# Attention scores with the low key products in two row halves of TensorE, and a choice table built from two small ones

## The reference

```
s_c   = q @ kcmp  - slope * dist      # 127 compressed keys, softmax, gives the importance of blocks
sel   = top 8 of 32 blocks of 64 keys # first block, own block and the one before are forced
s_sel = q @ k     - slope * (t - key) # softmax over the chosen blocks, key <= t
s_win = q @ k     - slope * (t - key) # softmax over a window of 512 keys
o     = gate0 * o_cmp + gate1 * o_sel + gate2 * o_win
```

## Time and profile before

| | us |
|---|---|
| median of 3 runs | 4977.47 |
| range of the runs | 4975.93 to 4987.32 |
| the profiled execution's own time | 4984.44 |
| its span, first to last instruction | 4982.9 |
| TensorE busy in the span | 4327.2 (87%) |
| VectorE busy | 2748.0 (55%) |
| GpSimd busy | 729.3 (15%) |
| attention, from 2022.4 to 3077.3 us of the span | 1054.9 |

### The profile page before, as it was taken

The page is one execution under the profiler, slowest core; times in us unless marked ns, Lnnn a source line. Parts: engine busy times, 40 slices in busy tenths (PEclk is TensorE's granted clock), DMA queues, the critical chain, the costliest instruction groups (busy, mean ns, idle before and its releaser), DMA issues. The chain is left out here.

```text
span 4982.9 us, 66879 instructions
## 1 busy us (share of the span) xinstructions
PE 4327.2 (87%) x24608; PEld 3592.7 (72%) x24609; DVE 2748.0 (55%) x4353; ACT 2039.0 (41%) x3193; POOL 729.3 (15%) x599
## 2 busy tenths in 40 slices
PE   6999999999999995788888876799635999999699
PEld 5887887888788773566666764688534888888577
DVE  2655655556567562576666654443225654557465
ACT  2433332233223221455555553101225655557465
POOL 0111111111122130211111110000012100001110
PEclk9999999999999997899999986899657999999899
DMA  4332322233222214000000001423217865669742
GB/s 138 108 87 74 107 81 62 86 109 87 65 74 61 67 43 104 25 11 14 17 15 17 14 22 55 140 94 115 92 59 293 314 249 214 245 256 344 286 145 98
DMA packets 440438, 558.72 MB, mean 112 GB/s; under 512 B 38908, under 2 KB 299004, under 8 KB 439148
## 3 DMA queue, kind: packets, MB, share of 16 engines
q1 hardware_dynamic: 387892, 451.51, 27.6%
q0 software_dynamic: 19072, 59.86, 3.2%
q10 hardware_dynamic: 33232, 44.10, 2.7%
HBM read 445.05 MB, written 110.35 MB: 111 GB/s over the span
## 5 line engine op out<-in xcount | busy, mean ns | idle before, releaser
L434 POOL TENSOR_TENSOR fr_Lm<-fr_M,fr_join 128x512 f32<-128x512 f32 x224 | 370.9, 1673 | 1493.2 <-DVE fr_M L1043 963.4
L462 PE MATMUL fr_fb<-fr_hT_h,fr_w_h 128*128 128x512 f32 (+1 forms) x1312 | 528.3, 403 | 16.6 <-DVEq L1004 10.8
L462 PE MATMUL fr_fb<-fr_hT_r,fr_w_h 128*128 128x512 f32 (+1 forms) x1312 | 527.4, 402 | 0.0
L462 PE MATMUL fr_fb<-fr_hT_h,fr_w_r 128*128 128x512 f32 (+1 forms) x1312 | 526.3, 401 | 0.0
L855 DVE TENSOR_TENSOR fr_w_r<-fr_w_raw,fr_w_h 128x1024 fp32r<-128x1024 f32 (+1 forms) x164 | 209.6, 1278 | 409.7 <-ACT fr_w_h L683 409.4
L1781 DVE TENSOR_TENSOR aq_p_lo<-aq_t_bank,aq_p_hi 128x512 fp32r<-128x512 f32 x412 | 281.4, 690 | 271.5 <-ACT aq_p_hi L1671 270.1
L1671 ACT CAST aq_p_hi<-aq_t_bank 128x512 fp32r<-128x512 f32 x412 | 238.9, 585 | 377.5 <-PE aq_t_bank L1585 375.4
L707 ACT COPY fr_zs<-fr_fb 128x512 f32<-128x512 f32 (+1 forms) x148 | 87.0, 588 | 585.0 <-PE fr_fb L462 584.6
L462 PEld LDWEIGHTS fr_fb<-fr_hT_h,fr_w_h 128*128 128x128 f32 (+1 forms) x1312 | 246.9, 188 | 74.7 <-DVEq L1004 11.3
L134 PE MATMUL ex_gu<-ex_gate_w,ex_xT 128*128 128x512 f32 x1176 | 288.3, 401 | 11.5 <-DVE ex_xT L2407 11.4
L134 PE MATMUL ex_yps<-ex_down_w,ex_hidT 128*128 128x512 f32 x1176 | 287.6, 400 | 2.6 <-DVE ex_hidT L2423 2.6
(11 more groups left out here) (438 smaller groups left out, 9957.8 us busy)
## 6 DMA issues: line engine op xcount, KB each, us to landing
ex_raw<-in_w_exp_gate_up SPq DMA_DIRECT2D x64, 2048.0 KB, 10.9
fr_w_raw<-in_w_in SPq DMA_DIRECT2D x160, 512.0 KB, 3.8
ex_raw<-in_w_exp_down SPq DMA_DIRECT2D x32, 2048.0 KB, 11.1
s_z<-fr_zs SPq DMA_DIRECT2D x160, 256.0 KB
s_rows<-ex_y ACTq DMA_DIRECT2D x50, 512.0 KB, 4.3
mx_mg<-s_z SPq DMA_DIRECT2D x16, 1024.0 KB, 7.8
fr_zc<-s_z SPq DMA_DIRECT2D x15, 903.0 KB, 6.8
fr_x_t<-in_x SPq DMA_DIRECT2D x16, 512.0 KB, 4.8
```

The costliest lines, as they stand in the source:

```text
L434: pool.tensor_tensor(Lm[:, g, :, :], M[:, 4 * g:4 * g + 4, 0, :], join[:, lev:lev + 1, :].to_broadcast([P, HG, CH]), ALU.mult).then_inc(l_ ...
L462: ins = pe.matmul(bank[0:cols_, :], (w_h, w_h, w_r)[p][:, k, c, 0:cols_].bitcast(F32R), (hT_h, hT_r, hT_h)[p][:, c, :].bitcast(F32R), star ...
```

## The change

It does four things. (1) The scores of a run are cut into two halves of equal width, one for each PSUM bank, where before they were cut into pieces of 512 and a remainder. (2) The products with `k_hi` stay over 128 rows. Those with `k_lo` are taken over 64 rows, with the rounded queries only: the first half of the keys from partitions 0 to 63, the second from 64 to 127, so that (q_lo)(k_lo) is no longer computed and the two products use different row halves of the array and different banks. (3) They need the rounded queries in all 128 partitions: a new tile `q_hh`, for which `take_q` makes one more rounding copy (64x1024). (4) The long table `t_sel` goes. `bias` now adds `sel` to a row of 32 numbers (`base`), adds that to a 128x64 table (`near`), and masks the last 128 keys by a select. VectorE's `mask` reads the two banks as two halves.

```diff
+            q_hh = st.sb("q_hh", [P, 2, G, R, P])
...
-                    pool.tensor_copy(whole(q_s, every).bitcast(F32R), raw(every)).then_inc(q_high, 1)
-                    pool.wait_ge(q_high, o + 1)
-                    pool.tensor_tensor(whole(q_s, rest).bitcast(F32R), raw(rest), whole(q_s, rest), ALU.subtract).then_inc(q_ok, 1)
+                    pool.tensor_copy(whole(q_hh, every).bitcast(F32R), raw(every)).then_inc(q_high, 1)
+                    pool.tensor_copy(whole(q_s, top_).bitcast(F32R), raw(top_)).then_inc(q_high, 1)
+                    pool.wait_ge(q_high, 2 * o + 2)
+                    pool.tensor_tensor(whole(q_s, rest).bitcast(F32R), raw(rest), whole(q_hh, rest), ALU.subtract).then_inc(q_ok, 1)
...
+                    pool.tensor_tensor(base[:, 0:blocks], ramp[:, N_SEL - blocks:N_SEL], sel[:, f % SELS, 0:blocks], ALU.add).then_inc(base_ok, 1)
+                    pool.wait_ge(base_ok, 2 * f + 1)
                     pool.tensor_tensor(tg[:, 0:keys].rearrange("p (n b) -> p n b", n=blocks),
-                                       t_sel[:, S - t * P:S - t * P + keys].rearrange("p (n b) -> p n b", n=blocks),
-                                       sel[:, f % SELS, 0:blocks].rearrange("p (n o) -> p n o", o=1).to_broadcast([P, blocks, SEL_BLOCK]),
-                                       ALU.add).then_inc(tg_ok, 1)
+                                       near[:, :].rearrange("p (o b) -> p o b", o=1).to_broadcast([P, blocks, SEL_BLOCK]),
+                                       base[:, 0:blocks].rearrange("p (n o) -> p n o", o=1).to_broadcast([P, blocks, SEL_BLOCK]),
+                                       ALU.add).then_inc(base_ok, 1)
+                    pool.wait_ge(base_ok, 2 * f + 2)
+                    pool.affine_select(out=tg[:, t * P:keys], in_=tg[:, t * P:keys], compare_op=ALU.is_ge, fill=NEG, base=0,
+                                       pattern=[[-1, P]], channel_multiplier=1).then_inc(tg_ok, 1)
...
-                step(pool.iota(t_sel[:, :], [[1, w]], base=-S, channel_multiplier=-1, allow_small_or_imprecise_dtypes=True))
-                masked(t_sel[:, :], [[-1, w]], S, 1, NEG)
+                step(pool.iota(near[:, :], [[1, SEL_BLOCK]], base=0, channel_multiplier=-1, allow_small_or_imprecise_dtypes=True))
+                step(pool.iota(ramp[:, :], [[SEL_BLOCK, N_SEL]], base=P - S, channel_multiplier=0, allow_small_or_imprecise_dtypes=True))
...
-                    key = F.low(u) * P + at
-                    for c in range(0, wide, 512):
-                        size = min(512, wide - c)
-                        dst = s_bank[:, i % 2, c:c + size]
-                        for n, k in enumerate((k_hi, k_lo)):
-                            ins = pe.matmul(dst, q_s[:, t % 2, g, h, :].bitcast(F32R),
-                                            k[:, b, g, key + c:key + c + size].bitcast(F32R), start=n == 0, stop=n == 1)
+                    key, half = F.low(u) * P + at, wide // 2
+                    for c in range(2):
+                        pe.matmul(s_bank[:, i % 2, 512 * c:512 * c + half], q_s[:, t % 2, g, h, :].bitcast(F32R),
+                                  k_hi[:, b, g, key + c * half:key + (c + 1) * half].bitcast(F32R), start=True, stop=False)
+                    for c in range(2):
+                        own = slice(c * HD, (c + 1) * HD)
+                        ins = pe.matmul(s_bank[:, i % 2, 512 * c:512 * c + half], q_hh[own, t % 2, g, h, :].bitcast(F32R),
+                                        k_lo[own, b, g, key + c * half:key + (c + 1) * half].bitcast(F32R), start=False, stop=True)
                     ins.then_inc(s_made, 1)
...
-                    dve.tensor_tensor_reduce(out=sc_of(u)[:, h, at:at + wide], in0=s_bank[:, i % 2, 0:wide], in1=table,
+                    dve.tensor_tensor_reduce(out=halves(sc_of(u)[:, h, at:at + wide]),
+                                             in0=s_bank[:, i % 2, :].rearrange("p (b n) -> p b n", b=2)[:, :, 0:wide // 2], in1=halves(table),
```

More of the change, by code:

```diff
@@ L1388, in stage_nsa @@
             QF, Y = 3, F.Y_RING
-            t_sel, t_win, t_cmp = st.sb("t_sel", [P, S + P]), st.sb("t_win", [P, WK]), st.sb("t_cmp", [P, 256])
+            t_win, t_cmp = st.sb("t_win", [P, WK]), st.sb("t_cmp", [P, 256])
+            near, ramp, base = st.sb("near", [P, SEL_BLOCK]), st.sb("ramp", [P, N_SEL]), st.sb("base", [P, N_SEL])
             rows_ok = st.sb("rows_ok", [P, 1])
@@ L1414, in stage_nsa @@
                 st.sem(n) for n in ("s_made", "s_read", "exp_ok", "turned", "hi_ok", "lo_ok", "pv_made", "ot_ok"))
-            misc_made, misc_read, cexp_ok, inv_ok, pc_ok, imp_ok, sel_ok, tg_ok, y_ok, vec = (
+            misc_made, misc_read, cexp_ok, inv_ok, pc_ok, imp_ok, sel_ok, tg_ok, y_ok, vec, base_ok = (
                 st.sem(n) for n in ("misc_made", "misc_read", "cexp_ok", "inv_ok", "pc_ok", "imp_ok", "sel_ok",
-                                    "tg_ok", "y_ok", "vec"))
+                                    "tg_ok", "y_ok", "vec", "base_ok"))
             y_out = st.lasting_sem("y_out", Z["whole"])
@@ L1475, in take_q @@
                     whole = lambda a, rows: a[rows, k, :, :, :].rearrange("p g h t -> p (g h) t")
-                    every, rest = slice(0, P), slice(HD, P)
+                    every, top_, rest = slice(0, P), slice(0, HD), slice(HD, P)
                     raw = lambda rows: q_raw[rows, :, :, :].rearrange("p g h t -> p (g h) t")
-                    pool.tensor_copy(whole(q_s, every).bitcast(F32R), raw(every)).then_inc(q_high, 1)
-                    pool.wait_ge(q_high, o + 1)
-                    pool.tensor_tensor(whole(q_s, rest).bitcast(F32R), raw(rest), whole(q_s, rest), ALU.subtract).then_inc(q_ok, 1)
+                    pool.tensor_copy(whole(q_hh, every).bitcast(F32R), raw(every)).then_inc(q_high, 1)
+                    pool.tensor_copy(whole(q_s, top_).bitcast(F32R), raw(top_)).then_inc(q_high, 1)
+                    pool.wait_ge(q_high, 2 * o + 2)
+                    pool.tensor_tensor(whole(q_s, rest).bitcast(F32R), raw(rest), whole(q_hh, rest), ALU.subtract).then_inc(q_ok, 1)
                     pool.wait_ge(q_ok, o + 1)
@@ L1496, in bias @@
                         pool.wait_ge(s_read, F.run_end[F.at[before]])
+                    pool.tensor_tensor(base[:, 0:blocks], ramp[:, N_SEL - blocks:N_SEL], sel[:, f % SELS, 0:blocks], ALU.add).then_inc(base_ok, 1)
+                    pool.wait_ge(base_ok, 2 * f + 1)
                     pool.tensor_tensor(tg[:, 0:keys].rearrange("p (n b) -> p n b", n=blocks),
-                                       t_sel[:, S - t * P:S - t * P + keys].rearrange("p (n b) -> p n b", n=blocks),
-                                       sel[:, f % SELS, 0:blocks].rearrange("p (n o) -> p n o", o=1).to_broadcast([P, blocks, SEL_BLOCK]),
-                                       ALU.add).then_inc(tg_ok, 1)
+                                       near[:, :].rearrange("p (o b) -> p o b", o=1).to_broadcast([P, blocks, SEL_BLOCK]),
[4 more added lines that the diff above has]
+                                       pattern=[[-1, P]], channel_multiplier=1).then_inc(tg_ok, 1)
                 take_q(NT - 1)
-                w = S + P
                 step(pool.iota(t_win[:, :], [[1, WK]], base=-WINDOW, channel_multiplier=-1, allow_small_or_imprecise_dtypes=True))
@@ L1758, in event @@
                         combine(n, t, k)
+                halves = lambda row: row.rearrange("p (b n) -> p b n", b=2)
                 def mask(i, u, h, at, wide):
```

## The result

| | before | changed |
|---|---|---|
| median, same chip, 4 runs each | 4976.7 | 5054.32 us |
| range | 4973.06 to 4987.32 | 5049.25 to 5065.95 us |
| ratio, 95% interval | | 1.0156 [1.0132, 1.0179] |

The changed kernel is 1.56% slower (+77.6 us). The forecast was +38 us, with the range up to 5062. The direction and the range held, the size did not: half of the loss was missing. The profiled execution took 5049.25 us (span 5047.7), 64.8 us of span over that of before. The other 13 us are no part of the change: the profiled execution of before lay 8 us over this median, and the one here lies 5 us under its own.

The account below looks back on a forecast made before the run. TensorE, busy 87% of the span, was taken to set the pace in SEL units and VectorE's masks to lead in WIN units. 33 us for scores plus 5 for GpSimd on 4977.47 gave 5015 us, range 4960 to 5062.

Parts of the forecast that it names:

- The round trip of 0.38 us: TensorE, each score run: going from 128 rows to 64 and back costs 0.38 us, ends 0 and 0.76.
- felt in full: Runs scored in SEL units, where TensorE is full: all 20 us of added work lengthen the time.
- a fifth: 16 WIN units of wide runs, 1.6 us added in each: a fifth of 25 us is felt, 5 us.
- grows by under 0.5: Sign in the new profile: the WIN unit of 16.4 us gets longer by less than 0.5 us.
- 21.0 or more: Sign in the new profile: the SEL unit for t = 12 that lasts 20.6 us lasts at least 21.0.
- put at 5 us: GpSimd's added query copy (+1.1 us each) and longer table (+0.75 us) together cost 5 us, taken from 9.
- 4 us for five or six late tables: VectorE's first wide mask of a SEL unit waits for five or six of 32 tables: 4 us (0 to 24).
- A mean PEclk of 0.91 is 18% of the attention at half clock, which I leave in the rounding: Attention: TensorE's half-clock time got no term of its own in the sum.
- the low clock spreads: Rival, attention: fewer columns and more gaps lower PEclk from 0.91 to 0.87, giving 5057 us; chance 0.11.
- The low products in series: Rival, score runs: the low pair doesn't run side by side, 47 us on top, about 5055 us; chance 0.04.
- the nearly free switch: Rival, score runs: row halves join without a drain, 33 us faster, 4944 us; chance 0.13.
- the absorbed change: Rival, attention: longer runs only fill TensorE's waits, a fifth of 60 us felt, 4985 to 4992 us; chance 0.15.

Follow-up runs that it names:

- e_switch: e_low128 with a tiny pair of 16-key products over the two row halves added behind each run; ratio to the kernel before 1.0206.
- e_low128: Changed kernel with low products over all 128 rows again, still in two even halves, `q_hh` made but not read; ratio to the kernel before 1.0039.
- e_win64: Changed kernel with row halves only in the runs of WIN units, the other low products over 128 rows; ratio to the kernel before 1.0084.
- e_sel64: Changed kernel with row halves only in the runs of SEL units, the other low products over 128 rows; ratio to the kernel before 1.0088.
- e_table: Kernel before with the new table alone, scores and queries as before; ratio to the kernel before 1.0017.
- e_series: Changed kernel with both low products taken from the upper 64 rows, so they run one after the other; ratio to the kernel before 1.0304.
- e_nolow: Changed kernel without any low products, scores from high keys alone; ratio to the kernel before 1.0023.
- e_fill: e_even with 448 filler products, four and three ahead of TensorE's waits for the exponential and for turned outputs; ratio to the kernel before 1.0032.
- e_even: Kernel before with runs over 512 keys cut in two even halves, all 128 rows, old table; ratio to the kernel before 0.9985.
- e_tabeven: e_even with the new table added, all products over 128 rows and no `q_hh`; ratio to the kernel before 1.0010.
- e_fill3: e_even with 120 filler products, only where its trace shows TensorE waiting 1 us or more; ratio to the kernel before 0.9966.

## Why the prediction was half right

**The mechanism held, and so did the work.** Pairs start together, a run of 640 takes 0.83 us instead of the 0.8 forecast, weigh's second product comes 0.34 us later (0.33). The round trip of 0.38 us is 0.40 in e_switch. Against the kernel before, the +38 of the changed kernel less 5 for the table and 0 to 3 for the copy leave 30 to 33 us for the scores, where I had 33. In the aligned traces the SEL units with t from 8 grow by 0.43 us at an equal clock, 6.9 us together, and four runs at 0.11 in each of the 16 units make 7.0.

Part of this is luck. Over e_low128, whose runs of 640 are in even halves already, a run of 640 costs 0.22 us more by the same sum (0.89 against 0.67), which is 0.88 for the four of a SEL unit with t from 8. The aligned traces of e_low128 and the changed kernel give 0.56. The WIN runs cost +18 us there (e_win64), where 31 was the price if felt in full; the SEL runs +10 (e_sel64), where I had 13. So the work in SEL units was not "felt in full"; the even halves gave back less than forecast too (8 us, and 0.21 in place of 0.44 in such a unit), and the two misses nearly cancel.

The WIN units with t from 8 grow by 0.65 us. Half of it is the late table, as unit (11,1) showed: +0.47 for the table alone, +0.31 for the row halves alone. So "a fifth" of their 1.6 us held for the row halves, and "grows by under 0.5" was wrong (16.44 to 17.20) since the table delays these units, too; the SEL forecast "21.0 or more" can be read only from a unit without the lower clock, and there (12,0) has 21.70, where it had 21.29.

**GpSimd** was put at 5 us. The table costs 5 without the clock (8 with it), the copy 3 or nothing. Its two prices came out as forecast, 4.4 and 4.5 us. Its 4 us for five or six late tables came out as some 0.35 us in each of the 16 WIN units with t from 8 (aligned traces of before and e_table), 5.6 us. Even halves give back 8 us, and cutting narrow runs takes 4; neither was a term by itself.

**The step that failed** is the sentence "A mean PEclk of 0.91 is 18% of the attention at half clock, which I leave in the rounding": the time at half clock was taken as unchanged. It rose from 205 to 276 us in the profiled attention, and from 764 to 885 us in the mean execution. 121 us at 0.33 are 40 us (at 0.42: 51), which leaves 38 (27) of the 77.6 for all the rest, and for that I had 38. So the term put at nothing was worth half of the loss. That the rest agrees to the microsecond is luck, with 12 us on either side of the measured loss. The case "the low clock spreads" had this price nearly to the microsecond (0.87 and 5057; it came out as 0.88 and 5054), but it stood there as a rival with 0.11, as if either the work or the clock could come. They come together, and the work that I forecast was no reason for the clock to stay. The low products in series, the nearly free switch and the absorbed change are refuted by e_series, e_switch and the ratio.

**What stays open** is what decides when TensorE is given the lower clock. It is lower in a kernel that issues fewer products (e_nolow, 0.84), where it falls more often, in one that is busier but streams over one row half (e_series, 0.82), where it stays down for longer, and higher with fillers (e_fill, 0.96). Most falls stand behind a wait, but the same wait can go with a fall or without one: ahead of unit (12,1) TensorE waits 1.72 us before, 1.82 in e_even and 1.84 in e_tabeven, and only in e_even the clock falls there (0.79 for the unit, 1.00 in the two others). These runs don't give a rule, and I don't know how much of the 0.36% for cutting narrow runs is such a chance of timing; 14 of its 18 us go with 43 us more at half clock. The slope of 0.33 is a correlation within kernels; that e_fill3 gains as it says (expected 15 us for 45, measured 9) speaks for it, but its interval holds zero as well; the unit (12,1) at both clocks, with the same products, is the firmer sign.

## What to carry to other kernels

Before trading full-height products for packed ones, count the round trips between tiling modes: at 0.4 us each they cost as much as some 890 columns at 0.45 ns, and the halves saved 512 in a run of 1024 keys and fewer in all others. If PEclk is under 1 in the stretch that is changed, the time at half clock is a term of the sum with a price (here 0.33 to 0.42 us for each us), and a change that takes columns away may raise it, so put a bound on it from the start. Filling TensorE's waits is worth a try only where the trace shows them: 120 products in waits of 1 us or more gave the fastest kernel (a gain over e_even as small as its interval), 448 without that choice made it slower.

## What the hardware showed that I had not expected

- Halving the score products (e_nolow against e_low128) made the kernel only 0.16% faster (8 us), while its time at half clock rose from 800 to 921 us.
- A pair of only 16 columns over row halves costs 0.40 us; the way in and out does not get cheaper when there is nothing to do between.
- Taking one row half for both low products lowered PEclk from 0.88 to 0.82 while TensorE's busy share rose from 86 to 90%. The clock fell as often (33 times) and stayed down for 12.6 us in the mean in place of 7.7, once for 20.5 us without any idle time of TensorE.
